# Adaptive-norm modulation chunks moved between stages, router products by token tile, two tiles gathered early, residual sums on GpSimd

## What is computed

```python
mod = silu(cond) @ w_ada + b_ada                  # two conditions; 6 parts of 2048 columns
sh1, sc1, gt1, sh2, sc2, gt2 = split(mod, 6)
h = rmsnorm(x, g_pre_mix) * (1 + sc1) + sh1
y = mixer(h)                                      # h @ w_in; gated linear attention | order-2 long convolution; @ w_out
x = x + gt1 * rmsnorm(y, g_post_mix)
h = rmsnorm(x, g_pre_ffn) * (1 + sc2) + sh2
y = moe(h)                                        # router: best of 4 groups, best 2 of its 4 experts
x = x + gt2 * rmsnorm(y, g_post_ffn)
```

## Time and profile before

| | us |
|---|---|
| median of 3 runs | 1619.06 (1616.66 to 1621.87) |
| profiled execution, time | 1618.71 |
| profiled execution, span of the trace | 1616.9 |
| PE busy | 1392.7 (86%) |
| DVE busy | 744.0 (46%) |
| ACT busy | 238.9 (15%) |
| POOL busy | 76.6 (5%) |
| moved by DMA | 421.92 MB |

### The profile page before, as it was taken

The page is one execution under the profiler, slowest core; times in us unless marked ns, Lnnn a source line. Parts: engine busy times, 40 slices in busy tenths (PEclk is TensorE's granted clock), DMA queues, the critical chain, the costliest instruction groups (busy, mean ns, idle before and its releaser), DMA issues.

```text
span 1616.9 us, 13844 instructions
## 1 busy us (share of the span) xinstructions
PE 1392.7 (86%) x5196; PEld 644.3 (40%) x5196; DVE 744.0 (46%) x1245; ACT 238.9 (15%) x390; POOL 76.6 (5%) x127
## 2 busy tenths in 40 slices
PE   2679959999999899999999989589989887899780
PEld 0135524444555445555544434433333333333330
DVE  0135785885776887977873756600000000000005
ACT  0211220100011021111221001411101110111013
POOL 4000000000001000000000000000000000000001
PEclk9799979999999999999999999789989989999995
DMA  9996246675559643122326733999989999999985
GB/s 332 414 358 208 95 146 227 232 244 188 170 176 335 202 142 111 59 85 90 125 97 241 241 135 107 417 348 414 399 335 394 403 403 406 401 406 384 408 357 202
DMA packets 131199, 421.92 MB, mean 261 GB/s; under 512 B 8130, under 2 KB 73893, under 8 KB 113253
## 3 DMA queue, kind: packets, MB, share of 16 engines
q1 hardware_dynamic: 118100, 375.78, 61.4%
q0 software_dynamic: 6656, 32.61, 6.1%
q10 hardware_dynamic: 6384, 12.73, 2.2%
HBM read 409.53 MB, written 23.09 MB: 268 GB/s over the span
## 4 chain that ended last, share of the span: by engine, by line
PE 59%; DMA 21%; DVE 13%; issue 3%; ACT 3%; ACTq 1%; POOLq 0%; SPq 0%; DVEq 0%; POOL 0%
PE ps L497 17%; PE ps L494 14%; DMA s_mem<-in_w_exp_gate 12%; PE ps L823 11%; DMA s_mem<-in_w_ada 7%; PE ps L843 6%; DVE s_mem L1439 4%; DVE s_mem L1604 2%; PE ps L441 1%; PE ps L663 1%; DMA s_mem<-in_hy_freq 1%; DVE s_mem L1576 1%; PE ps L614 1%; PE ps L423 1%; PE ps L625 1%
## 5 line engine op out<-in xcount | busy, mean ns | idle before, releaser
L1439 DVE SCALAR_TENSOR_TENSOR s_mem<-s_mem,s_sT 128x512 f32<-128x512 f32 x480 | 339.4, 748 | 56.8 <-DMA s_mem<-in_w_ada 45.4
L494 PE MATMUL ps<-s_mem 128*128 128x384 f32 x1024 | 343.1, 492 | 1.1 <-DVE s_mem L1470 1.1
L497 PE MATMUL ps<-s_mem 128*128 128x512 f32 x768 | 339.8, 601 | 0.7 <-ACT s_mem L1256 0.7
L823 PE MATMUL ps<-s_mem 128*64 128x512 f32 x1152 | 261.6, 611 | 34.8 <-DMA s_mem<-in_w_exp_gate 34.2
L494 PEld LDWEIGHTS ps<-s_mem 128*128 128x128 f32 x1024 | 193.5, 192 | 142.5 <-issue 18.3
L497 PEld LDWEIGHTS ps<-s_mem 128*128 128x128 f32 x768 | 146.3, 193 | 184.8 <-issue 183.7
L823 PEld LDWEIGHTS ps<-s_mem 128*64 128x64 f32 x1152 | 88.2, 141 | 205.4 <-issue 204.5
L1868 DVE TENSOR_TENSOR s_mem<-s_mem,ps 64x512 f32<-64x512 f32 x18 | 12.2, 680 | 325.4 <-ACT s_mem L1330 325.4
L843 PE MATMUL ps<-s_mem 128*64 128x512 f32 x576 | 152.4, 690 | 9.3 <-DVE s_mem L1870 9.3
L843 PEld LDWEIGHTS ps<-s_mem 128*64 128x64 f32 x576 | 45.5, 157 | 103.0 <-issue 91.1
L1152 ACT ACTIVATE s_mem<-ps 128x512 f32<-128x512 f32 (+1 forms) x61 | 34.4, 581 | 338.3 <-PE ps L497 172.4
(11 more groups left out here) (258 smaller groups left out, 931.9 us busy)
## 6 DMA issues: line engine op xcount, KB each, us to landing
s_mem<-in_w_ada SPq DMA_DIRECT2D x128, 512.0 KB, 5.0
s_mem<-in_w_exp_up SPq DMA_DIRECT2D x32, 2048.0 KB, 33.0
s_mem<-in_w_exp_gate SPq DMA_DIRECT2D x32, 2048.0 KB, 25.8
s_mem<-in_w_exp_down SPq DMA_DIRECT2D x32, 2048.0 KB, 29.5
s_mem<-in_w_in SPq DMA_DIRECT2D x24, 2048.0 KB, 8.8
s_mem<-in_w_ada SPq DMA_DIRECT2D x16, 2048.0 KB, 12.6
s_mem<-in_w_out SPq DMA_DIRECT2D x8, 2048.0 KB, 8.1
y_slots<-s_mem ACTq DMA_DIRECT2D x36, 256.0 KB, 11.2
```

What stands on the lines that cost most here:

```text
L494: m = mm(ps[:, banks[m_], 0:TOK], v[:, k, m_ * P:(m_ + 1) * P], hT[:, kk, :], start=(kk == 0), stop=(kk == KT - 1))
L497: m = mm(ps[:, banks[m_], :], hT[:, kk, m_ * P:(m_ + 1) * P], v[:, k, :], start=(kk == 0), stop=(kk == KT - 1))
L823: m = mm(ps[half, 0, :], hgT[:, kh * 8 + k, :], weights(e, 2 * kh + which)[:, k, :], start=(kh + k == 0), stop=(kh * 8 + k == KT - 1), ski ...
L1439: v.op(ve.scalar_tensor_tensor(out=o, in0=w, scalar=scale, in1=o, op0=ALU.mult, op1=ALU.add), S("piece_used") if last else None)
```

## The change

1. **Chunks.** `ADA_SUMS`, `PIECES_AFTER` and `SUMS_AT` are new, and so are the places of `run` and `mod_chunk` in DVE's program. Steps of `ada_steps` done before each point, before and after: ahead of the reads of `la` 16 and 26; ahead of the `ks` products 32 and 44; ahead of head 0 112 and 136; ahead of the first filter taps 180 and 200; ahead of the output projection's reads 215 and 240. `ada_sum(1)` stays behind k's second half, `ada_sum(2)` to `(8)` and `ada_sum(9)`, `(10)`, `(11)` each come one or more halves earlier, and 12 leaves the output projection for hy10. Chunk 1 gets a place of its own; chunks 11 and 12 both lie at `AT_MOD`.
2. **Second norm.** DVE's last product of the third tile (`weigh_rows(3, 2)`) moves into `norm_tile(1)`.
3. **Router.** The product is made tile by tile, the first between the transposes of tiles 1 and 2. `pairs_ready` is signalled ahead of the five small steps that make the pair weights.
4. **First gather of rows.** It reads its indices from `idx_i` itself, without the copy to `idx_now`.
5. **Tail.** Two tiles instead of one are gathered early (rows of experts 0 to 14) and completed late, and the early gathers wait for the last weight load but one instead of the last. The third tile is weighed on POOL. For tiles 0 and 1 ACT scales by the inverse root and POOL adds the residual; for tile 2 DVE does both in two halves of 1024 columns, each stored by its own DMA.

```diff
-        ADA_SUMS = {("q", 1): 0, ("k", 1): 1, ("v1", 0): 2, ("v1", 1): 3, ("g0", 0): 4, ("g0", 1): 5, ("g1", 0): 6,
-                    ("hy00", 0): 7, ("hy01", 0): 8, ("hy01", 1): 9, ("hy11", 0): 10, ("hy12", 0): 11,
-                    ("wo0", 1): 12, ("wo1", 1): 13, ("wo2", 0): 14, ("wo3", 0): 15}
-        PIECES_AFTER = {1: 4, 2: 2, 4: 4, 5: 1, 6: 4, 7: 3, 8: 4, 9: 4, 10: 3, 11: 1, 12: 2, 13: 3, 14: 2, 15: 3,
-                        16: 3, 17: 3, 18: 1, 20: 1, 22: 1, 24: 1, 25: 2, 27: 2, 28: 4, 29: 4, 30: 2}
+        ADA_SUMS = {("q", 1): 0, ("k", 1): 1, ("v0", 1): 2, ("v1", 0): 3, ("v1", 1): 4, ("g0", 0): 5, ("g0", 1): 6,
+                    ("g1", 0): 7, ("g1", 1): 8, ("hy00", 1): 9, ("hy01", 1): 10, ("hy02", 0): 11, ("hy10", 0): 12,
+                    ("wo1", 0): 13, ("wo2", 0): 14, ("wo3", 0): 15}
+        PIECES_AFTER = {1: 2, 2: 4, 3: 3, 4: 3, 5: 2, 6: 3, 7: 4, 8: 3, 9: 5, 10: 4, 11: 3, 12: 2, 13: 3, 14: 2, 15: 3,
+                        16: 2, 17: 4, 18: 1, 20: 1, 22: 1, 24: 1, 25: 2, 27: 2, 28: 3, 29: 1}
-        SUMS_AT = [{3: AT_ARENA, 5: AT_ARENA, 7: AT_ARENA, 8: AT_ARENA + 3072, 10: AT_ARENA + 22016,
-                    13: AT_ARENA + MIX, 15: AT_ARENA + MIX}.get(m, AT_MOD) for m in range(CHUNKS)]
+        SUMS_AT = [{1: AT_ARENA + 2 * MIX, 3: AT_ARENA, 5: AT_ARENA + 1536, 7: AT_ARENA, 8: AT_ARENA + 1536,
+                    10: AT_ARENA + 1536, 14: AT_ARENA + MIX}.get(m, AT_MOD) for m in range(CHUNKS)]
...
+            turn_h2(0)
+            turn_h2(1)
+            route(0)
+            turn_h2(2)
+            route(1)
+            route(2)
...
-            i = LOADS_A_EXPERT * NE - 1
+            i = LOADS_A_EXPERT * NE - 2
             pool.wait_ge(S(f"w{i % len(MOE_SLOTS)}"), 16 * (i // len(MOE_SLOTS) + 1))
-            gather_y(early_i, range(1))
+            gather_y(early_i, range(2))
...
+            pool.wait_ge(S("y_gathered20"), 16)
+            g.op(nc.gpsimd.tensor_scalar(yga[2][0], yga[2][0], wpair[:, 0, 2:3], None, ALU.mult), S("last_weighed"))
+            for t in range(2):
+                pool.wait_ge(S("z_scaled"), t + 1)
+                g.op(nc.gpsimd.tensor_tensor(yga[t][0], yga[t][1], x_sb[:, t, :], ALU.add), S("rows_added"))
...
+                if t < 2:
+                    act.wait_ge(S("root_ready"), t + 1)
+                    a.op(A(yga[t][1], yga[t][1], ACT.Copy, scale=stat[:, 32 + t:33 + t]), S("z_scaled"))
...
-            run(16)
+            run(26)
 
             for d in range(2):
                 for h in range(HEADS):
...
+            run(4)
             dve.wait_ge(S("pool_const"), 1)
...
-            run(16)
+            mod_chunk(0)
+            run(14)
             wait_read(dve, "act", "q_3")
...
-            mod_chunk(0)
-            for m in range(2, 7):
-                run(16)
-                mod_chunk(m - 1)
-                if m == 5:
-                    mod_row(2)
+            mod_chunk(1)
+            run(20)
+            mod_chunk(2)
+            run(16)
+            mod_chunk(3)
+            mod_row(2)
+            run(16)
+            mod_chunk(4)
+            run(20)
+            mod_chunk(5)
+            run(16)
+            mod_chunk(6)
+            run(4)
...
             short_conv(0, 1, 3)
-            mod_chunk(9)
-            run(16)
+            mod_chunk(10)
+            run(12)
+            mod_chunk(11)
...
             mod_row(4)
-            run(11)
+            run(16)
             dve.wait_ge(S("in_gate"), 16 * NT)
             for nb in range(4):
                 if nb == 1:
-                    mod_chunk(12)
-                    run(14)
-                if nb == 2:
-                    mod_chunk(13)
-                    run(14)
-                    mod_chunk(14)
-                if nb == 3:
                     for _ in ada:
                         pass
+                if nb == 3:
+                    mod_chunk(14)
                     mod_chunk(15)
...
-            combine(0)
-            for t in range(1, NT):
-                combine(t)
-                add_residual(t - 1)
-            add_residual(NT - 1)
+            for t in range(2):
+                combine(t)
+                inverse_roots(32 + t, 1)
+                v.sync()
+                dve.sem_inc(S("root_ready"), 1)
+            combine(2)
+            inverse_roots(34, 1)
+            for half in range(2):
+                c = slice(half * (D // 2), (half + 1) * (D // 2))
+                v.op(ve.scalar_tensor_tensor(out=yga[2][0][:, c], in0=yga[2][1][:, c], scalar=stat[:, 34:35],
+                                             in1=x_sb[:, 2, c], op0=ALU.mult, op1=ALU.add), S("out_ready"))
```

98 lines of the change are left out of this document (58 added, 40 removed).

## The result

| | before | after |
|---|---|---|
| median of 7 runs, us | 1619.15 (1616.66 to 1621.87) | 1624.63 (1622.99 to 1626.58) |
| profiled execution, span, us | 1616.9 | 1621.6 |
| PE busy, us | 1392.7 | 1395.9 |
| POOL busy, us | 76.6 | 97.0 |

The ratio of after to before is 1.0038, 95% interval 1.002 to 1.0056. The median became 5.5 us longer; the forecast was 14.2 us shorter, with a range that ended at 1613.5.

A forecast was written before the change was run, and what follows sets the result against it. PE bounds the middle and the weight stream the experts. Gains of 10.6 us (chunks), 3.0 (norm and router) and 0.6 (tail) sum to 14.2 us, from the median 1619.06 to 1604.9 us; range 1592 to 1613.5.

The forecast's parts named there:

- What goes: PE's waits at ada_sum(1), hy01's transposes, the filter taps and the output projection vanish: 19.6 + 2.0 + 8.2 + 8.5 = 38.3 us gained.
- The step on bank 7 behind mod_chunk(9): At hy01's transposes PE's 2.0 us wait goes, because 24 more steps are done before head 0.
- What comes at `la`: 26 steps ahead of DVE's la reads delay PE's third la product by 9.9 us; 12.7 us added with low-clock work.
- slow window: PE's work at a lower granted clock for about 6 us behind a wait; 2.8 us charged for a new one.
- Nothing is late there: On to the attention heads, each chunk is complete 13 to 20 us ahead of its sum, so no new wait.
- DVE falls behind: Rival, 9%: pieces cost 3 us more in each of seven halves, putting 8 us on PE at ada_sum(7): 1612.9.
- The taps: At the first filter taps PE waits 12.2 us for eight steps behind ada_sum(11); 15.0 us added with low-clock work.
- The router: Second norm and router: 5.0 us saved up to the first gather, of which 3.0 us (0 to 5) counted.
- The rival that the router's gain is not had: At the first gather the DMA queues are full, so no gain: 1607.9, inside the forecast's range; no chance given.
- The tail: After the experts: early gathers of two tiles and POOL's scale and two adds gain 0.6 us (0.6 to 4.9).
- the exclusion: Rival, 17%: in the tail POOL's passes and DVE's two-SBUF-input operations do not overlap, 3.7 us worse: 1608.6.
- GpSimd setting the end: Rival, 4%: POOL's tail scale and adds make it slower than before from an add of 12.5 us; 1627.9 at 14.

The follow-up runs named there:

- e10: Kernel after with chunk 12's own place and four, three and two pieces behind loads 1, 2 and 3: 1596.21 us, ratio 0.9875 to before.
- e14: Kernel with places and pieces repaired, minus second-condition sums after each chunk's first step; single execution: first turn of h2 at 860.0 us instead of 871.8.
- e5: Kernel after with one table entry more, a place of its own for chunk 12's running sum: 1609.79 us, ratio 0.9958 to before.
- e8: Kernel after with unused GpSimd and DVE operations of 128x2048 float32 added behind its end, alone and in pairs; only the operations' times are reported.
- e9: Kernel before with the router's part, and one 2 MB weight load held back until the first rows are gathered: ratio 1.0003 to before.
- e2: Kernel before with only the second norm, router product by tile, later pair weights and first gather without its copy: ratio 0.9994.

## Why the prediction was wrong, by its own steps

*What goes.* Right, with sizes: the interval with `ada_sum(1)` became 18.0 us shorter for 19.6 forecast, and the output projection from its third half on 11.1, of which 2.0 are two sums that moved ahead of it, so 9.1 for 8.5. The step on bank 7 behind mod_chunk(9), 2.0 us, failed: PE waits there 3.8 us, now behind mod_chunk(10), of which the three steps ahead of the last `short_conv` are a part. "DVE has no late piece there" was read off a count of steps, not off DVE's time.

*What comes at `la`.* The mechanism was right (the load of k ahead of piece 2), the term 2.4 us too small, from two errors. Counted from q's start, the third product came 13.8 us later than before and not 9.9, since pieces 4 and 6 came 1.6 and 2.4 us late as well; piece 4 was taken to be in time, and piece 6 was left out of the working. The slow window behind the wait cost 1.4 us and not 2.8. e10 shows that all but 0.9 us of the term is SP's order.

*"Nothing is late there."* This is the step that failed by most: 10.1 us, as much as the whole shortfall of the chunks (9.9), since the other misses, +2.4, +1.6, +2.4 and -6.5, cancel. In the 10.1 us are the wait of 4.1 us at `ada_sum(7)` with slower products behind it (granted clock 0.54 from 381 to 384 us), the 3.8 us at L607, and 1.0 us that is no loss, the sum that moved into this interval. It held each chunk against its sum at 13 to 20 us of slack. In the trace chunk 7 is complete at 375.2 us, where chunk 8 begins, 1.8 us ahead of the time at which PE could have taken it (381.12 - 4.08 = 377.0), and the sum also needs bank 7, whose reader mod_chunk(6) stood four steps later. So a slack of 13 us was one of 1.8, and what PE waited for was the bank. The rival "DVE falls behind" put 8 us on PE for 9%; of its mechanism this much is in the trace:

```profile
DVE s_mem L1469 <- DMA s_mem<-in_w_ada: 15.4, 6, 3.8
DVE s_mem L1464 <- DMA s_mem<-in_w_ada: 4.6, 2, 2.7
```

These are DVE's waits on pieces from 195 to 400 us, 20.0 us in eight. That is the 3 us in each of seven halves that I had called harmless, and not the 21 us beyond it that the rival asked for. So the waits were no longer than allowed; the slack that should have taken them was not there. With about half the work (e14) and the same loads in the same order PE's waits vanish, so it is DVE's work plus these waits that has no slack.

*The taps.* Right: a wait of 11.75 us for 12.2 forecast, released by mod_chunk(11). The interval grew by 9.2 for 6.8, and 1.0 of the difference is a sum that moved into it. The slow window behind the wait cost less than the 2.8 us: the twelve products took 4.62 us, against 3.67 in e5. e5 shows that it is the shared place, worth 14.3 us by itself.

*The router.* The steps up to the gather came out (issued 6.3 us earlier, 4.5 of them beyond the stage's own earlier start, for 5.0 forecast), but the 3.0 us were not had. My reason was idle DMA time around the gather; what counts is what was full ahead of it:

```profile
1045.44 1.03 POOL L1094 DMA_INDIRECT s_mem<-h_rows,s_idx_i  x1 [54.18 <-issue]
...
1054.72 1.59 PE L799 MATMUL ps<-s_base,s_mem 64*128 64x64 f32 x12 [12.76 <-DMA s_mem<-h_rows,s_idx_i]
```

From the gather's issue to PE's first use it takes 9.3 us; before it took 4.7, from 1051.74 to 1056.48. The rival that the router's gain is not had was right.

*The tail.* The step that failed is the overlap. Both prices were off too, but they cancel: the scale was 3.6 us in the forecast and is 5.44, the sum of two tiles was 5.4 and is 4.49, and one scale and two sums are 14.4 us either way. The tail came out 6.9 us worse than forecast. Along POOL, from PE's last block on: the third tile's rows were there after 17.5 us, for 15.7 in the forecast, 1.9 us late (why was not found). The three operations took 18.3 us (7.28 and 11.02) and not 14.4, since DVE held the scale for 1.8 and the second sum for 2.0. From POOL's end to the end of the span it was 8.1 us and not 7.0, since the halves were held by the second sum. So the exclusion, a rival at 17%, is what happens, in another order than it said (combine(1) was first and the scale waited). Seen from DVE, combine(2) waits 2.79 us for the scale, is held some 4.2 us by the first sum, and the halves 1.6 us by the second, 8.6 us together. The memset of 1.81 us was the nearest row and no measure: a copy is near it (1.89), a scale is three times as long.

SBUF — State Buffer of the Trainium skill, "Who interferes with whom", says that DVE and GpSimd lock each other out for a whole instruction when DVE has two SBUF inputs and GpSimd reads SBUF, or when a DVE operation of one input runs in a two-port mode, and that a DVE instruction with at most one SBUF input outside those modes does not contend. The three pairs with the sum agree (13.78, 9.53 and 9.26 us); the pair with one SBUF input does so if its 1.29 us for 2048 columns, for 2.29 with a PSUM input, is such a two-port mode, which no row names. The pair of the scale with two SBUF inputs agrees in part (3.3 us of 5.4). Had I believed the rule rather than looked for a row that shows it, the sum would have held the 3.7 us of the rival. GPSIMD Engine Reference of the Trainium skill, "Elementwise — side-by-side cycle accounting", gives 4497 ns for the sum, and the trace 4.49 us. In "Engine selection" the same page of the Trainium skill calls operations of one input roughly line-rate for GpSimd; the copy at 1.89 us agrees, the scale at 5.44 us, slower than the sum, does not, and here the measurement decides.

*The sum and the range.* Forecast were gains of 10.6, 3.0 and 0.6 us; measured are a gain of 0.7 (with a scatter of some 2.5), nothing, and a loss of 6.3. Each of the three lay at or past the bad end of its own bounds, and the range allowed for one of them at a time. The side that was left out at 4%, GpSimd setting the end, had its condition at a sum of 12.5 us. The loss came at a sum of 4.5, since the 13.6 us that it was set against were not there and the exclusion, which it left out, was.

## What to carry to other kernels

- When background work on an engine is moved ahead, add up that engine's whole time up to each deadline, its waits for data included, and look at every semaphore of the deadline (here the bank's last reader beside the chunk). A slack read off counts of steps is none; and mending one order only moves the wait, as long as the engine itself is late.
- A running sum that shares its place with the last one ties two loops together, and a piece behind a big load in one queue costs what the load costs. Both were a few table entries, worth 14.3 and 11.4 us here by the profiles, and both are found by asking what stands ahead of the first instruction that is needed.
- Before elementwise work goes to GpSimd beside DVE on the path that sets the end, see which DVE operations lie beside it. In these runs those that read PSUM ran free; for the others take the sum of both engines' times, not the larger. And a gather that is issued earlier was worth nothing here behind a full queue.

## What the runs showed of the hardware

- GpSimd, 128x2048 float32: scale by a column 5.44 us, by a constant 5.36 us, sum of two tiles 4.49, copy 1.89. The scale is slower than the sum.
- Beside GpSimd's sum of 4.49 us, DVE operations of two SBUF inputs stand still for 4.4 us, and so do those of one SBUF input, which alone take 1.29 us for 2048 columns (e8). Where DVE was first it was GpSimd's scale that became longer, by 2.1 us. A DVE operation with one SBUF and one PSUM input runs free beside GpSimd (four in 9.26 us, 2.29 alone).
- With one 2 MB load fewer ahead of it in the queues, PE's first use of the gathered rows came 5.1 us behind the gather's issue instead of 9.0 (e9 and e2).
- Four products that take 1.53 us at a granted clock of 1.00 took 2.90 us behind PE's wait of 12.6 us at `la`, and a granted clock of 0.50 stands in the profile from 172 to 176 us.
